# Scores of 64-feature heads: two heads at a time, one in each row half of TensorE's array, and attention rounds by pairs of heads

## The chip, the cores and the metric

The kernel runs on one core of one Trainium2 chip. The metric is the device time of one execution in microseconds (us). A core has TensorE (PE in the profile; PEld is its weight loads), VectorE (DVE), ScalarE (ACT), GpSimd (POOL) and SyncE (SP, whose queue issues the weight transfers).

## What is computed

The reference is two model blocks behind one another on x of 256 tokens by 1024 features, all in float32. Block one has two layers of: a gated norm, a mixer, a gated norm, a feed-forward part (width 2816). Block two has two layers of: half a feed-forward part, a mixer, attention on 256 memory tokens, half a feed-forward part. What matters here are the mixers whose heads have 64 features:

```python
# block one, both layers: 8 heads "slc" and 8 heads "win" share the queries; with 256 tokens
# both come to causal attention. 8 heads "moba" are causal attention too
s = einsum(q, k) * 64 ** -0.5        # 256 x 256 per head
p = masked_softmax(s, mask)
o = einsum(p, v)
# block two, layer 0: differential half (8 score maps, chunked mask) and stick half (8 heads)
p = p[:, :n_h] - lam * p[:, n_h:]
z = einsum(q, k) * 64 ** -0.5
later = cumsum(log_keep, reverse) - log_keep
w = where(strict, exp(log_sigmoid(z) + later), 0)
```

The other attention loops (block two, layer 1: 16 heads of 96 features; the memory attention: 4 heads of 128 features) are not by pairs in either kernel.

## The kernel before, in words

All five engines run one program each, written out by hand in program order; semaphores tie them. Every weight matrix is streamed in panels of 128 x 2048 elements through `ring` (3 slots). ScalarE copies a panel to the rounded part "hi" of `parts` (2 slots, L705), VectorE makes the rest "lo" by a subtraction (L2272, 128x2048), and TensorE multiplies hi by hi, hi by lo and lo by hi (L1489, L1495, L1497). A panel may be written to `parts` once TensorE has used the panel two before it. Panels of `w_ada` in between are not multiplied on TensorE: VectorE adds them up, four multiply-adds a panel (`ada_add`, L2281, `feat<-ring,scol,feat`), and TensorE sums the columns (`ada_cols`, L1507).

**The attention loops.** `head_steps` (L1674) gives TensorE three pieces per head: `scores` (two plain float32 products, of 128x128 and 128x256 outputs, L1686), `turn` (three 128x128 transposes of the probabilities, L1698) and `weighted` (probabilities by values, L1711). The loop of the first mixers (L1869) has 27 rounds. Round i does scores(i), turn(i-2), weighted(i-3) and then two steps of the weight products beside it (`more`, UNITS = 2; a step is 12 products of 512 columns or 24 of 256, and four steps use up a panel). Behind some rounds come extra pieces: the compressed branch (2, 5, 6), transposes of queries, keys and outputs (8, 14, 21), `ada_cols` (5, 9, 13, 17, 24, 26). The differential loop (L2029) has 11 such rounds with 2 or 3 steps. The stick loop (L2049) does in round i the score z(i) (L2053, L2055), the sums "later" of head i-1 (L2063 to L2065), the weighted values of head i-3 (L2078) and two steps.

**VectorE** in round i does first `masked(i)` (L2500: takes the scores out of PSUM, adds the mask, finds the row extreme `nmax`, which frees the bank), and then the rest of its round in program order: in even rounds the four multiply-adds of an ada panel and the lo of a weight panel, in some odd rounds head norms, rotations and branch sums. **ScalarE** in round i copies the transposed probabilities to `prob_t` (`turned_copy`), does `exps(i)`, and in odd rounds empties PSUM banks and makes a panel's hi.

**Banks and buffers.** Scores and transposes share two PSUM banks, `ATT = (0, 1)`; `open_bank` takes the one opened longest ago and waits until its last user has freed it. In the kernel before, scores take bank 0 and transposes bank 1 in every round. Masked scores lie in `shifted` (3 slots), transposed probabilities in `prob_t` (2 slots).

Heads n and n+1 of a pair have their queries and keys in the partitions 0 to 63 and 64 to 127 of the same tile:

```python
    q=nq_t[HD * g:HD * g + HD, j, :], k=k_t[HD * g:HD * g + HD, :]
    for i in range(HEADS + LAG + 1):
        if i < HEADS:
            scores(i)
```

## Time and profile before

| | us |
|---|---|
| median of 3 runs (lowest, highest) | 2058.11 (2057.46, 2058.28) |
| span of the profiled execution | 2056.4 |
| TensorE busy, matmuls | 2007.2 (98%) |
| TensorE busy, weight loads | 1779.3 (87%) |
| VectorE busy | 1463.2 (71%) |
| ScalarE busy | 1093.2 (53%) |
| mixer of block one, layer 0, attention loop | about 93 to 220 |
| the same, layer 1 | about 545 to 671 |
| differential loop, stick loop | about 1146 to 1190, 1198 to 1250 |

The profiled execution's own time is known by its span only, 2056.4 us; the runs' median is 1.7 us above it, about what lies around a span. In the rows below a line has the start in us from the span's start, the busy time of a merged group, the engine, the source line, the operation, output and inputs with their shapes, and the number of instructions. A plain float32 product shows as two matmuls, so one head's scores are four. In brackets stands the idle time of the engine ahead of the group and what ended it.

### The profile page before, as it was taken

What the parts mean: (1) busy time and instruction counts of PE and PEld (TensorE: products, weight loads), DVE (VectorE), ACT (ScalarE), POOL (GpSimd) and SP (SyncE); (2) the same over time, 40 slices, a digit from 0 to 9 for tenths busy, and PEclk for the clock granted to TensorE, in tenths of its full rate; (3) what the DMA queues carried; (4) which work ended last, traced back from release to release, by engine and by line L of the source; (5) the groups of instructions that cost most, each with busy time, mean ns of one, the idle gap of its engine ahead of it and who ended that gap; (6) DMA issues with size and microseconds to landing.
All of it is one profiled execution on the core that took longest, in us unless ns stands there. A gap on an engine that the chain in (4) does not pass through costs nothing. (4 is left out here: it accounts for less than half of the span.)

```text
span 2056.4 us, 32208 instructions
## 1 busy us (share of the span) xinstructions
PE 2007.2 (98%) x12956; PEld 1779.3 (87%) x12956; DVE 1463.2 (71%) x2322; ACT 1093.2 (53%) x1732; POOL 23.9 (1%) x46
## 2 busy tenths in 40 slices
PE   7999999999999999999999999999999999999999
PEld 4879988888889988898889779888898899899888
DVE  5888678867786686657766767677667757767774
ACT  3555545534655555545544665655445546855552
POOL 1001000000001000000000000000000000000000
PEclk9999999999999999999999999999999999999999
DMA  9555558867454466565556433455555554235554
GB/s 315 173 186 203 184 176 266 276 235 218 162 179 167 135 205 219 175 194 184 185 185 204 144 103 124 137 189 186 174 191 188 185 169 152 93 123 156 188 179 134
DMA packets 266212, 372.23 MB, mean 181 GB/s; under 512 B 8400, under 2 KB 160336, under 8 KB 266064
## 3 DMA queue, kind: packets, MB, share of 16 engines
q1 hardware_dynamic: 264736, 368.91, 55.1%
q8 instruction: 103, 1.69, 0.3%
q10 hardware_dynamic: 1328, 1.26, 0.2%
q14 instruction: 45, 0.37, 0.1%
HBM read 369.09 MB, written 1.05 MB: 180 GB/s over the span
## 5 line engine op out<-in xcount | busy, mean ns | idle before, releaser
L2272 DVE TENSOR_TENSOR parts<-ring,parts 128x2048 fp32r<-128x2048 f32 (+2 forms) x304 | 675.7, 2223 | 398.8 <-ACT parts L705 397.9
L705 ACT ACTIVATE parts<-ring 128x2048 fp32r<-128x2048 f32 (+2 forms) x304 | 565.5, 1860 | 577.6 <-PE psum L1497 317.1
L1497 PE MATMUL psum<-h,parts 128*128 128x512 f32 x1920 | 675.6, 397 | 0.0
L1495 PE MATMUL psum<-h,parts 128*128 128x256 f32 x1920 | 538.9, 281 | 0.3
L1497 PEld LDWEIGHTS psum<-h,parts 128*128 128x128 f32 x1920 | 360.5, 188 | 86.9
L1495 PEld LDWEIGHTS psum<-h,parts 128*128 128x128 f32 x1920 | 362.3, 189 | 2.5 <-DVE parts L2272 2.5
L1489 PE MATMUL psum<-h,parts 128*128 128x256 f32 (+1 forms) x2088 | 265.0, 285 | 4.5 <-DVE h L2281 2.0
L1489 PEld LDWEIGHTS psum<-h,parts 128*128 128x128 f32 (+1 forms) x2088 | 253.9, 190 | 7.3 <-issue 5.0
L1489 PE MATMUL psum<-parts,h 128*128 128x512 f32 (+1 forms) x864 | 204.4, 388 | 4.8 <-DVE parts L2272 3.4
L1489 PEld LDWEIGHTS psum<-hid_hl,parts 128*128 128x128 f32 x1584 | 189.5, 190 | 2.4 <-DVE parts L2272 2.4
L1489 PE MATMUL psum<-hid_hl,parts 128*128 128x256 f32 x1584 | 190.9, 283 | 0.8 <-DVE parts L2272 0.6
L1489 PEld LDWEIGHTS psum<-parts,h 128*128 128x128 f32 x864 | 155.1, 189 | 36.8 <-issue 4.6
L1497 PE MATMUL psum<-hid_hl,parts 128*128 128x512 f32 x528 | 186.8, 397 | 0.0
L1495 PE MATMUL psum<-hid_hl,parts 128*128 128x256 f32 x528 | 148.8, 282 | 0.1
L705 ACT ACTIVATE tok<-psum 128x512 f32<-128x512 f32 (+3 forms) x156 | 90.3, 579 | 70.9 <-PE psum L1497 61.8
L1497 PEld LDWEIGHTS psum<-hid_hl,parts 128*128 128x128 f32 x528 | 99.1, 188 | 24.3
L1495 PEld LDWEIGHTS psum<-hid_hl,parts 128*128 128x128 f32 x528 | 99.5, 188 | 0.6 <-DVE parts L2272 0.5
L705 ACT ACTIVATE scores_area<-scores_area,nmax 128x256 f32<-128x256 f32 (+1 forms) x160 | 72.2, 456 | 36.5 <-DVE nmax L2500 36.0
L2272 DVE TENSOR_TENSOR tok<-psum,tok 128x512 f32<-128x512 f32 x120 | 82.0, 683 | 1.9 <-ACT tok L705 1.7
L705 ACT ACTIVATE scores_area<-psum 128x384 f32<-128x384 f32 (+1 forms) x80 | 40.0, 499 | 77.3 <-PE psum L1698 76.9
L1686 PE MATMUL psum<-feat 64*128 64x128 f32 (+4 forms) x320 | 73.5, 351 | 1.5 <-DVE nmax L2500 0.9
L2500 DVE CUSTOM_DVE_ANT_0 scores_area<-psum,const,sums 128x128 f32<-128x128 f32 (+1 forms) x96 | 37.3, 426 | 52.5 <-PE psum L1686 48.3
(259 smaller groups left out, 2124.0 us busy)
## 6 DMA issues: line engine op xcount, KB each, us to landing
ring<-in_w_ada SPq DMA_DIRECT2D x48, 1024.0 KB, 5.3
ring<-in_w_ffn_in SPq DMA_DIRECT2D x88, 512.0 KB, 4.9
ring<-in_ffn_w_gate SPq DMA_DIRECT2D x88, 512.0 KB, 4.0
ring<-in_ffn_w_up SPq DMA_DIRECT2D x88, 512.0 KB, 5.0
ring<-in_w_in SPq DMA_DIRECT2D x36, 1024.0 KB, 5.1
ring<-in_ffn_w_down SPq DMA_DIRECT2D x32, 1024.0 KB, 5.1
ring<-in_w_ffn_out SPq DMA_DIRECT2D x16, 1024.0 KB, 5.1
ring<-in_ffn_w_down SPq DMA_DIRECT2D x16, 768.0 KB, 4.5
```

What stands on the lines that cost most here:

```text
L705: act.activation(out, in_, func, **kw).then_inc(*sig(name, *keys))
L1489: mm = pe.matmul(out, left, right, start=start and n == 0, stop=stop and n == 2, skip_group_check=True)
L1495: pe.matmul(bank[:, 0:S], wt_hl[1], act[:, 0, :], start=start, stop=False, skip_group_check=True)
L1497: return pe.matmul(bank.rearrange("p (a s) -> p a s", a=2), wt_hl[0], act, start=False, stop=stop, skip_group_check=True)
L1686: mm = pe.matmul(b[:, a:c], head["q"][:, P * t:P * t + P], head["k"][:, 0:c - a], start=True, stop=True)
L2272: dve.tensor_tensor(out, a, b, op).then_inc(*sig(name, *keys))
L2500: dve.tensor_tensor_reduce(to, of, add, times, 3.0e38, ALU.add, ALU.min, nmax[:, n % 3, t:t + 1]).then_inc(*sig("dve_nmax", *keys))
```

## The change

`scores` for heads of 64 features becomes `pair_scores`: it opens both `ATT` banks and issues the products of two heads alternately (first head 128 columns, second head 128, first 256, second 256). It runs in even rounds only. In a round the steps beside are divided: in even rounds both stand between the scores and `turn`, in odd rounds one ahead of `turn` and one behind `weighted`. `shifted` gets 4 slots in these loops and `nmax` 4 (the memory attention keeps 3 slots, by another division of the same area). ScalarE does `exps(i)` ahead of `turned_copy(i-2)`. The stick half issues z of two heads at a time. The loop of 96-feature heads keeps `scores`, with 4 slots and nothing else new.

```diff
-        shifted = scores_area[:, 0:3, :]
-        prob_t = scores_area[:, 3:5, :]
+        in_heads = scores_area.rearrange("p a n -> p (a n)")[:, 0:6 * 384].rearrange(
+            "p (a n) -> p a n", n=384)
+        shifted, prob_t = in_heads[:, 0:4, :], in_heads[:, 4:6, :]
...
+                    if i < HEADS:
+                        exps(heads[i], base + i,
+                             heads[i]["n"] + (8 if heads[i]["st"][0] == "win" else 0))
                     if LAG <= i < HEADS + LAG:
                         m = i - LAG
                         turned_copy(heads[m], base + m)
-                    if i < HEADS:
-                        exps(heads[i], base + i,
-                             heads[i]["n"] + (8 if heads[i]["st"][0] == "win" else 0))
...
+                def pair_scores(i):
+
+                    two = heads[i:i + 2]
+                    for key in (scores_need or {}).get(i, ()):
+                        pe.wait_ge(*at(key))
+                    banks = [open_bank(("scores", head["st"], head["i"]), ATT) for head in two]
+                    for t, (a, c) in enumerate(spans(two[0]["mask"])):
+                        for head, b in zip(two, banks):
+                            mm = pe.matmul(b[:, a:c], head["q"][:, P * t:P * t + P],
+                                           head["k"][:, 0:c - a], start=True, stop=True)
+                            if t:
+                                mm.then_inc(*sig("pe_scores",
+                                                 ("full", ("scores", head["st"], head["i"]))))
...
                 for i in range(HEADS + LAG + 1):
-                    if i < HEADS:
+                    if i < HEADS and i % 2 == 0:
                         scores(i)
+                    ahead = UNITS if i % 2 == 0 or i == 23 else 1
+                    advance(more, ahead)
                     if LAG <= i < HEADS + LAG:
                         turn(i - LAG)
-                    if i == 23:
-                        next(more, None)
                     if i > LAG:
                         weighted(i - LAG - 1)
-                    for n in range(UNITS - (i == 23)):
-                        next(more, None)
-                        if i == 2:
-                            compressed_scores(n)
+                    advance(more, UNITS - ahead)
...
                 for i in range(8 + LAG + 1):
-                    if i < 8:
+                    if i < 8 and i % 2 == 0:
                         scores(i)
+                    ahead = beside_diff(i) if i % 2 == 0 else 1
+                    advance(more, ahead)
...
-                    advance(more, beside_diff(i))
+                    advance(more, beside_diff(i) - ahead)
...
+                    if i < 8 and i % 2 == 0:
+                        banks = [open_bank(("z", i + j), stick if i else ATT) for j in range(2)]
+                        for k in range(2):
+                            for j in range(2):
...
-                if n >= 3:
-
-                    dve.wait_ge(*at(("full", ("turn", *att_log[n - 3]))))
+                if n >= slots(st):
+
+                    dve.wait_ge(*at(("full", ("turn", *att_log[n - slots(st)]))))
```

TensorE's program in the rounds 10 and 11 of layer 0, before. `h,parts` are steps, `psum<-feat` the scores, `psum<-const,scores_area` the transposes, `psum<-tok,scores_area` the weighted values; `dve_nmax` is the semaphore of `masked`:

```order
L1686 MATMUL psum<-feat 128x128 [waits dve_nmax]
L1686 MATMUL psum<-feat 128x256
L1698 MATMUL psum<-const,scores_area 128x128 [waits act_probs,act_copied]
L1698 MATMUL psum<-const,scores_area 128x128 [waits act_probs]
L1698 MATMUL psum<-const,scores_area 128x128
L1711 MATMUL psum<-tok,scores_area 128x64 [waits act_copied]
L1711 MATMUL psum<-tok,scores_area 128x64 x2
L1489 MATMUL psum<-h,parts 128x256 [waits dve_lo]
L1489 MATMUL psum<-h,parts 128x256 x23
L1686 MATMUL psum<-feat 128x128 [waits dve_nmax]
L1686 MATMUL psum<-feat 128x256
L1698 MATMUL psum<-const,scores_area 128x128 [waits act_probs,act_copied]
```

And the pair of rounds in the changed program:

```order
L1710 MATMUL psum<-feat 128x128 [waits act_copied]
L1710 MATMUL psum<-feat 128x128
L1710 MATMUL psum<-feat 128x256 x2
L1501 MATMUL psum<-h,parts 128x256 [waits dve_lo]
L1501 MATMUL psum<-h,parts 128x256 x23
L1724 MATMUL psum<-const,scores_area 128x128 [waits act_probs,dve_nmax]
L1724 MATMUL psum<-const,scores_area 128x128 [waits act_probs]
L1724 MATMUL psum<-const,scores_area 128x128
L1737 MATMUL psum<-tok,scores_area 128x64 [waits act_copied]
L1737 MATMUL psum<-tok,scores_area 128x64 x2
L1501 MATMUL psum<-h,parts 128x256 x12
L1724 MATMUL psum<-const,scores_area 128x128 [waits act_probs,dve_nmax]
```

The wait on `dve_nmax`, that is on `masked` having emptied the bank, has moved from the scores to the transposes: those of an even round need the pair's first head out of bank 0, those of an odd round its second head out of bank 1, and the scores now wait for ScalarE's copy (`act_copied`).

VectorE's program from `masked(8)` to `masked(9)` in the changed kernel. Its instructions stand in the same order as before in every round:

```order
L2530 ISA scores_area,nmax<-psum,const 128x256
L2530 ISA nmax 128x1
L2311 SCALAR_TENSOR_TENSOR feat<-ring,scol,feat 128x512 [waits dve_nmax,panel0]
L2311 SCALAR_TENSOR_TENSOR feat<-ring,scol,feat 128x512 [waits dve_ada] x3
L2302 TENSOR_TENSOR parts<-ring,parts 128x2048 [waits act_hi]
L2530 ISA scores_area,nmax<-psum,const 128x128 [waits pe_turned,pe_scores]
```

Nothing moved here: between the first and the second head of a pair VectorE still has the multiply-adds and the lo of a panel.

## Rows read from the trace of the kernel before

**Rows 1.** Profile page, part 1: busy time of each engine

```profile
PE 2007.2 (98%) x12956; PEld 1779.3 (87%) x12956; DVE 1463.2 (71%) x2322; ACT 1093.2 (53%) x1732; POOL 23.9 (1%) x46
```

**Rows 2.** Busy time by stretch: the mixer loops and the differential loop; columns named in the first line

```profile
core 0: us, PE busy (x) PEld busy (x) DVE busy (x) ACT busy (x) POOL busy (x), PEclk, DMA share, GB/s
93.00:220.00 127.00, 124.79 (x859) 107.27 (x858) 103.84 (x240) 69.23 (x169) 8.45 (x15) 1.00 0.56 193
545.00:671.00 126.00, 123.72 (x855) 106.83 (x854) 94.08 (x226) 69.76 (x170) 7.13 (x12) 1.00 0.49 168
1146.00:1190.00 44.00, 43.40 (x223) 33.58 (x221) 24.65 (x55) 27.82 (x64) 0.00 (x0) 1.00 0.43 144
```

**Rows 3.** Timeline, round 11 of layer 0: TensorE, and ScalarE's copy of the transposes

```profile
152.35 0.52 PEld L1686 LDWEIGHTS psum<-feat 64*128 64x128 f32 x4
152.35 0.92 PE L1686 MATMUL psum<-feat 64*128 64x128 f32 x4
153.20 0.55 PE L1698 MATMUL psum<-const,scores_area 128*128 128x128 f32 x3
153.59 0.78 PE L1711 MATMUL psum<-tok,scores_area 128*128 128x64 f32 x6
154.18 3.12 PE L1489 MATMUL psum<-h,parts 128*128 128x256 f32 x24
157.23 0.92 PE L1686 MATMUL psum<-feat 64*128 64x128 f32 x4
163.59 0.49 ACT L705 ACTIVATE scores_area<-psum 128x384 f32<-128x384 f32 x1 [2.62 <-PE psum L1698]
```

**Rows 4.** Timeline, TensorE: a head of 96 features in block two, layer 1

```profile
1762.16 0.82 PE L1686 MATMUL psum<-feat 96*128 96x128 f32 x4
1762.82 0.49 PE L1698 MATMUL psum<-const,scores_area 128*128 128x128 f32 x3
1763.15 0.78 PE L1711 MATMUL psum<-aux,scores_area 128*128 128x64 f32 x6
```

**Rows 5.** Timeline, VectorE, from `masked(12)` to `masked(13)` of layer 0

```profile
158.27 0.28 DVE L2500 CUSTOM_DVE_ANT_0 scores_area<-psum,const 128x128 f32<-128x128 f32 x1
158.82 0.08 DVE L2500 DVE_READ_ACCUMULATOR2_ANT nmax<- 128x1 f32 x1
159.01 3.12 DVE L2281 SCALAR_TENSOR_TENSOR feat<-ring,scol,feat 128x512 f32<-128x512 f32 x4
162.04 2.28 DVE L2272 TENSOR_TENSOR parts<-ring,parts 128x2048 fp32r<-128x2048 f32 x1
164.24 0.28 DVE L2500 CUSTOM_DVE_ANT_0 scores_area<-psum,const 128x128 f32<-128x128 f32 x1
```

**Rows 6.** Timeline, layer 0: VectorE's `masked(4)` and `masked(5)`, TensorE's scores(6)

```profile
113.94 0.29 DVE L2500 CUSTOM_DVE_ANT_0 scores_area<-psum,const 128x128 f32<-128x128 f32 x1 [1.98 <-PE psum L1686]
122.94 0.28 DVE L2500 CUSTOM_DVE_ANT_0 scores_area<-psum,const 128x128 f32<-128x128 f32 x1
123.49 0.08 DVE L2500 DVE_READ_ACCUMULATOR2_ANT nmax<- 128x1 f32 x1
123.63 0.92 PE L1686 MATMUL psum<-feat 64*128 64x128 f32 x4
```

**Rows 7.** Timeline, VectorE: an even round of layer 1 behind the last ada panel

```profile
641.88 2.28 DVE L2272 TENSOR_TENSOR parts<-ring,parts 128x2048 fp32r<-128x2048 f32 x1
646.00 0.35 DVE L2500 CUSTOM_DVE_ANT_0 scores_area<-psum,const,sums 128x128 f32<-128x128 f32 x1 [1.83 <-PE psum L1686]
```

**Rows 8.** Stick loop: z(6), z(5)'s bank, TensorE's wait, the stretch behind (rows 2's columns)

```profile
1229.13 0.70 PE L2053 MATMUL psum<-feat 64*128 64x256 f32 x2
1231.09 0.55 DVE L2272 TENSOR_TENSOR rot<-scores_area,psum 128x384 f32<-128x384 f32 x1
1232.38 0.93 PE L2063 MATMUL psum<-rot,const 128*128 128x256 f32 x2 [2.33 <-DVE rot L2272]
1232.30:1236.00 3.70, 3.62 (x14) 3.43 (x15) 3.54 (x8) 0.92 (x2) 0.00 (x0) 0.55 0.02 4
```

More of the change, by code:

```diff
@@ L299, in build @@
         rs = sb("rs", [P, 4, 8])
-        nmax = sb("nmax", [P, 3, TT])
+        nmax = sb("nmax", [P, 4, TT])
         sums = sb("sums", [P, 32, TT])
@@ L1693, in turn @@
                     b = open_bank(job, ATT)
-                    buf = shifted[:, (base + i) % 3, :]
+                    buf = shifted_of(head["st"], base + i)
                     for t, (a, c) in enumerate(spans(head["mask"])):
@@ L1710, in weighted @@
                         for n, o in enumerate(range(a, c, P)):
-                            mm = pe.matmul(head["o"][t], prob_t[:, (base + i) % 2, o:o + P],
+                            mm = pe.matmul(head["o"][t], prob_of(head["st"], base + i)[:, o:o + P],
                                            head["v"][n], start=n == 0, stop=o == c - P)
@@ L1714, in weighted @@
                         [("attended", head["st"])] if head["last"] else [])))
-                return scores, turn, weighted
+                return pair_scores if heads[0]["q"].shape[0] == HD else scores, turn, weighted
             pe.wait_ge(*at("loaded const"))
@@ L2049, in diff_mixer @@
                 for i in range(11):
-                    if i < 8:
-                        b = open_bank(("z", i), ATT if i < 2 else stick)
-                        r = slice(HD * (i % 2), HD * (i % 2) + HD)
-                        pe.matmul(b[:, 0:S], zk[r, i // 2, 0:P], zq[r, i // 2, :], start=True,
-                                  stop=True)
-                        pe.matmul(b[:, S:S + P], zk[r, i // 2, P:S], zq[r, i // 2, P:S],
-                                  start=True, stop=True).then_inc(
-                            *sig("pe_scores", ("full", ("z", i))))
+                    if i < 8 and i % 2 == 0:
+                        banks = [open_bank(("z", i + j), stick if i else ATT) for j in range(2)]
+                        for k in range(2):
+                            for j in range(2):
+                                r = slice(HD * j, HD * j + HD)
+                                mm = pe.matmul(banks[j][:, S * k:S * k + (P if k else S)],
+                                               zk[r, i // 2, P * k:P * k + P],
+                                               zq[r, i // 2, P * k:S], start=True, stop=True)
+                                if k:
+                                    mm.then_inc(*sig("pe_scores", ("full", ("z", i + j))))
                     if 1 <= i <= 8:
```

28 lines of the change are left out of this document (19 added, 9 removed).

## The prediction, as it was put on record

> **What bounds the kernel now.** I read the page's busy times first: TensorE's matmuls are busy for 98% of the span, VectorE 71%, ScalarE 53% [rows 1]. So a microsecond taken from TensorE counts as long as nothing else comes last. Then I read the busy times of three of the four loops that the change touches [rows 2]. In the loop of layer 0 TensorE is busy 124.8 of 127 us, but VectorE is busy 103.8, 82%, far over its mean; in layer 1 it is 94.1 of 126, in the differential loop 24.7 of 44. Last I read single rounds. A round of TensorE is 4.88 us (152.35 to 157.23): scores 0.85, transposes 0.39, weighted values 0.59, two steps 3.05 [rows 3]. VectorE is not in step with that. In an even round it has 0.63 of `masked`, then multiply-adds of 3.12 and a lo of 2.28, and only then `masked` of the next head: 158.90 to 164.24, 5.34 us in a row with no idle time [rows 5]. It holds because before, head 2m+1 has until the scores of head 2m+2.
>
> **What the change takes away: time in scores.** A head of 64 features takes 0.85 us from its first matmul to the transposes and 0.39 more to the weighted values, 1.24 in all [rows 3]; a head of 96 features with the same shapes takes 0.66 and 0.33, 0.99 [rows 4]. So entering and leaving the 64-row form costs 0.25 us, and about 0.09 more ahead of the first matmul in a merged row (my estimate from the same starts). One head in two no longer pays it, less 0.06 because a step and not a transpose follows: 0.28 us a pair. The four passes of a second head come on top, 0.66 if nothing overlaps. Its weight loads do not run beside each other: four loads are 0.52 busy, one load about 0.19, so they start 0.11 apart [rows 3]. If matmuls of different row halves may overlap, but start in order and each behind its load, the four passes of 128 columns still stand 0.11 apart; only of the four of 256 columns (0.22 each, from 0.66 less two of 0.11) two fall together. That gives 0.21. No row before shows two row halves in use at once, so the pair from its first matmul to its first step is bounded by 1.56 us (no overlap) and 1.0 us (one head and 0.15). I take **1.35**, the one that the rows of loads lead to. Where nothing waits, a pair saves 0.49 us, and 32 pairs (12 and 12, 4 differential, 4 stick) 15.7.
>
> By the Trainium skill (TensorE: Matmul & The Clock Gate, section The mechanism in Part 3) matmuls in different row groups start some 4 ns apart and run together; no row here shows it yet, and that is the end at 1.0.
>
> **What it adds: an earlier date for the second head.** The transposes of the odd round now go into bank 1, which holds the pair's second head until `masked(2m+1)`. From the pair's start T, TensorE asks for it at T + 1.35 + two steps 3.04 + transposes and values 0.93 + one step 1.52 = T + 6.84. Before, it asked at the second next scores, T + 9.75. VectorE sees the first head at T + 1.19 (last matmul of head one at T + 0.77, and 0.42 as between these two before) and has the second out at T + 1.19 + 0.63 + W + 0.64 + 0.05 = T + 2.5 + W, where W is its work in the even round. So **TensorE stalls as soon as W is over 4.3 us**, and W is 5.34 [rows 5]: a stall of 1.0 us, where 0.49 was won. Behind TensorE's wait on its queue stand the values, a step and the next pair, so VectorE gets its next first head late too; nothing makes the time good. ScalarE's copy of the transposes (0.49 [rows 3]) now stands behind `exps` of the late head; it is done 1.5 us after the turn starts, where the next pair asks after 2.4. That costs nothing, nor do the fourth slot and the new order on ScalarE; the DMAs are the same and on the same queue.
>
> Pair by pair, each W from VectorE's rows (delay against before, us):
> - Layer 0, pair 0-1: TensorE waits for `masked(1)` behind 5.1 us of work as before: 0. Pair 2-3: W 5.1, compressed scores beside: stall 1.1, delay 0.
> - Pair 4-5: W is 122.94 - 114.58 = 8.4 us, and scores(6) stood 0.06 behind `masked(5)` [rows 6]. Now the turn of round 5 stands there, and values, a step, `cmp turn` and `ada_cols`, 3.5 us, come behind it in place of ahead. Stall 4.2, delay 3.7.
> - Pairs 6-7, 8-9: the even rounds have 2.0 and 0.95 us of extra TensorE work, which cover W; delay falls to 2.4.
> - Pairs 10-11 to 22-23: W 5.3 to 5.8 in each, and 6.4 with `y_mix` in the last. Stalls of 0.9 to 1.4 (0.6 with the transposes of round 14), each less 0.49: +0.4, +0.6, +0.2, +1.0, +0.8, +1.0, +0.5. The loop ends 6.9 late.
> - Layer 1 is the same to round 17, 3.7 late there; behind the last ada panel W is 2.3 to 3.4 [rows 7], nothing stalls, and three pairs win 0.4 each: 2.4 late.
>
> Sum of the loops: +6.9 +2.4 = **+9.3 us**. In the same way it is +10.7 at 1.56 and +4.3 at 1.0.
>
> **Clock.** Behind a wait of 2.33 us the granted clock was 0.55 over the next 3.7 us, between its levels of 1.2 and 2.4 GHz [rows 8]. The two stalls of 4.2 us are longer. Such a stretch costs up to 1.7 us where TensorE is the bound; I take 1.5 each, **+3.0**.
>
> **Differential loop.** VectorE is busy 24.7 us in this loop's 10 rounds [rows 2], 2.5 a round with `masked` in it, so W stays under 4.3, and two or three steps cover it: nothing stalls, 4 x 0.49 = **-2.0** (-1.1 to -3.7).
>
> **Stick loop.** The first three pairs win about 1.4 us. The last z pair needs the bank of z(5), freed at about 1231.6 by 1231.09 and 0.55; z(6) alone was issued at 1229.13, ahead of the wait of 2.33 [rows 8]. It now stands behind it, 1.3 us of TensorE with a low clock: **0** (-1.5 to +1.5). The memory attention and the 96-feature loop change nothing.
>
> Sum: 9.3 + 3.0 - 2.0 + 0 = +10.3. The profiled span goes from 2056.4 to 2066.7, the median, 1.7 above it, from 2058.1 to **2068.4**. The case's own range: from 4.3 + 3.0 - 3.7 - 1.5 = +2.1 to 10.7 + 3.4 - 1.1 + 1.5 = +14.5, 2060 to 2073.
>
> **Rivals.**
> - *No overlap of the row halves*, so the change does only half of what it says: 1.56 a pair, +10.7 + 3.0 - 1.1 + 0.5 = +13, 2071. For it: no row shows an overlap. Against: nothing in the rows forbids it.
> - *Full overlap, as by the page named above*: 1.0 a pair. The loops give +4.3 (VectorE's chain remains), clock 3.0, differential -3.7, stick -1.5: +2.1, 2060, inside what cannot be told from no change.
> - *The other side: VectorE is in time.* The place is the turn of the odd round. If the second head is out before T + 6.8, because VectorE's work spreads into the idle time that it has ahead of `masked` elsewhere (1.83 us, for instance [rows 7]), every pair wins: -15.7 at 1.35, 2042; -9 with no overlap, 2049; with it in layer 1 and the late rounds alone, about -6, 2052. For it: VectorE is idle for 23 us of that loop [rows 2]. Against: its program order is fixed, and the idle time lies behind the second head, not ahead of it. It decides at W = 4.3 us.
>
> **Chances.** My case 0.40, no overlap 0.20, full overlap 0.14, VectorE in time 0.22, the rest (a new wait that I miss, slower still) 0.04. What a measurement can tell from no change is 0.2%, 4.1 us. Slower by more: 0.40 + 0.20 + 0.04, 0.64. Within: the full overlap, 0.14. Faster: 0.22. The range holds my case with its bounds and the milder half of the faster one: 2047 to 2073.
>
> **What would show it.** Right: in the loop of layer 0 TensorE's transposes wait for VectorE's `nmax` once in each pair, some 1 us each and about 4 us once in each layer, near round 5, with a half clock behind it; the loop ends some 7 us late; score pairs of about 1.3 us, the third and fourth loads ahead of the matmul; the differential loop 2 us shorter. Wrong: no wait of the transposes for VectorE; loops that end early; or pairs of 1.0 or 1.5 us, which tell the overlap. If VectorE's even rounds turn out shorter than 4.3 us, or the stalls are made good in the rounds 24 to 26, the forecast falls.

## The result, and the profile after the change

The changed kernel takes **2081.1 us** (median of four runs, 2077.7 to 2086.4), the kernel before on the same chip 2057.8 (2057.3 to 2058.3): a ratio of 1.0118 with a 95% interval from 1.0106 to 1.013. It is slower by 23.4 us, where 10.3 were forecast. The profiled execution took 2080.15 us, its span is 2078.3, 21.9 above the span before.

First the page's busy times, beside [rows 1], and the busy times of the three loops, beside [rows 2] (the same stretches on the clock of the span; the first line names the columns):

```profile
PE 1994.8 (96%) x12956; PEld 1778.5 (86%) x12956; DVE 1464.1 (70%) x2322; ACT 1094.7 (53%) x1732; POOL 23.7 (1%) x46
```

```profile
core 0: us, PE busy (x) PEld busy (x) DVE busy (x) ACT busy (x) POOL busy (x), PEclk, DMA share, GB/s
93.00:220.00 127.00, 112.44 (x788) 99.37 (x788) 95.41 (x226) 64.28 (x154) 8.36 (x15) 0.95 0.51 174
545.00:671.00 126.00, 113.38 (x765) 98.06 (x764) 90.87 (x226) 69.46 (x159) 7.04 (x12) 0.95 0.49 169
1146.00:1190.00 44.00, 40.52 (x207) 32.39 (x206) 35.77 (x70) 29.64 (x62) 0.00 (x0) 1.00 0.46 149
```

TensorE has 12.4 us less to do in all, although some of it ran at half clock, and takes 21.9 us longer over it. In the loop of layer 0 it is idle 14.6 us of 127, before 2.2, and its granted clock there is 0.95 on the mean, before 1.00.

A round of a pair, TensorE from pair 12-13 on; it answers to [rows 3]:

```profile
159.14 0.93 PE L1710 MATMUL psum<-feat 64*128 64x128 f32 x8
160.00 3.14 PE L1501 MATMUL psum<-h,parts 128*128 128x256 f32 x24
162.97 0.49 PE L1724 MATMUL psum<-const,scores_area 128*128 128x128 f32 x3
163.30 0.78 PE L1737 MATMUL psum<-tok,scores_area 128*128 128x64 f32 x6
```

Two heads now take 0.86 us from the first matmul to the step, as long as one took before. The eight matmuls of the group start in twos, 7 ns apart within a two, and the twos follow each other by 0.21, 0.11 and 0.21 us. The second head adds 0.01 us.

Now the turn of an odd round, which answers to [rows 5]: VectorE from `masked(14)` to `masked(15)` in layer 0, and TensorE's transposes behind it:

```profile
171.09 0.29 DVE L2530 CUSTOM_DVE_ANT_0 scores_area<-psum,const 128x128 f32<-128x128 f32 x1 [1.10 <-PE psum L1710]
171.95 0.49 DVE L2306 TENSOR_SCALAR feat<-ring,scol 128x512 f32<-128x512 f32 x1
172.47 2.98 DVE L2311 SCALAR_TENSOR_TENSOR feat<-ring,scol,feat 128x512 f32<-128x512 f32 x3
175.38 2.54 DVE L2302 TENSOR_TENSOR parts<-ring,parts 128x2048 fp32r<-128x2048 f32 x1
177.84 0.28 DVE L2530 CUSTOM_DVE_ANT_0 scores_area<-psum,const 128x128 f32<-128x128 f32 x1
178.53 0.55 PE L1724 MATMUL psum<-const,scores_area 128*128 128x128 f32 x3 [1.14 <-DVE nmax L2530]
```

And pair 4-5, against [rows 6]: the second head comes out 9 us behind the first.

```profile
112.39 0.29 DVE L2530 CUSTOM_DVE_ANT_0 scores_area<-psum,const 128x128 f32<-128x128 f32 x1 [2.11 <-PE psum L1710]
121.39 0.28 DVE L2530 CUSTOM_DVE_ANT_0 scores_area<-psum,const 128x128 f32<-128x128 f32 x1
122.09 0.79 PE L1724 MATMUL psum<-const,scores_area 128*128 128x128 f32 x3 [3.70 <-DVE nmax L2530]
```

The waits over the whole kernel (engine, line, what it waited for: us in total, times, the longest):

```profile
ACT scores_area L717 <- DVE nmax L2530: 89.1, 42, 5.1
PE psum L1724 <- DVE nmax L2530: 25.2, 18, 4.3
PE psum L1501 <- ACT aux L717: 7.2, 2, 3.6
```

The last of these is new in size: 7.2 us in two waits, one at the end of each block-one loop. The timeline there, layer 0; ScalarE has `exps` of head 23 late, then a table load, the gates' sigmoid and two copies, and TensorE's next step needs the bank that those copies free:

```profile
225.80 0.35 DVE L2530 CUSTOM_DVE_ANT_0 scores_area<-psum,const,sums 128x128 f32<-128x128 f32 x1 [0.17 <-DVE y_mix L2302]
226.60 0.40 ACT L717 ACTIVATE scores_area<-scores_area,nmax 128x128 f32<-128x128 f32 x1 [3.19 <-DVE nmax L2530]
227.98 1.28 ACT L717 ACT_TABLE_LOAD   x1
230.24 1.07 ACT L717 ACTIVATE aux<-psum 128x512 f32<-128x512 f32 x2
231.41 4.63 PE L1501 MATMUL psum<-y_mix,parts 128*128 128x256 f32 x24 [3.62 <-ACT aux L717]
```

Before, the same step waited 1.97 us in layer 0, and in layer 1 it hardly waited:

```profile
671.67 1.53 PE L1489 MATMUL psum<-y_mix,parts 128*128 128x256 f32 x11 [0.42 <-ACT aux L705]
```

Last, the clock. Three stretches of layer 0 in which TensorE was granted half its clock, 1.2 GHz in place of 2.4 (columns: TensorE busy, PEclk, DMA share, GB/s):

```profile
122.30:125.70 3.40, 3.40 (x14) 0.51 1.05 402
190.50:200.70 10.20, 10.20 (x50) 0.50 0.28 103
228.10:234.90 6.80, 3.50 (x16) 0.50 0.62 198
```

Before the change no stretch at half clock lay in the two loops of block one or right behind them; now there are seven, 40.8 us in all. The one at 122.3 stands behind the wait of 3.70 us. Ahead of the one of 10.2 us stands nothing but a row of short waits, 1.04, 1.21, 1.14 and 1.71 us, one in each pair.

Where the 21.9 us of the span are, measured between the first scores of each loop:

| | before | after | difference |
|---|---|---|---|
| start to the first scores of layer 0 | 93.6 | 91.9 | -1.7 |
| layer 0 to the first scores of layer 1 | 450.7 | 462.8 | +12.1 |
| layer 1 to the first differential scores | 602.1 | 613.9 | +11.8 |
| differential loop to the end | 910.1 | 909.7 | -0.3 |

The first line is no gain of the change: in the traces of this study it lies between 91.2 and 93.9 without regard to the kernel.

### The profile page after: what moved, and what is told of

It reads as the page before. It is cut to its first block, busy times and chain, and to the rows that moved or that the text cites. A ratio compares the mean times of both kernels' runs of the same rounds, so it can differ in the third digit from the quotient of the medians.

```text
span 2078.3 us, 32235 instructions
## 1 busy us (share of the span) xinstructions
PE 1994.8 (96%) x12956; PEld 1778.5 (86%) x12956; DVE 1464.1 (70%) x2322; ACT 1094.7 (53%) x1732; POOL 23.7 (1%) x46
## 4 chain that ended last, share of the span: by engine, by line
PE 74%; DVE 17%; ACT 5%; issue 3%; DMA 0%; DVEq 0%; ACTq 0%
PE psum L1501 29%; PE psum L1509 25%; PE psum L1507 13%; DVE parts L2302 6%; ACT parts L717 3%; DVE feat L2311 2%; PE psum L1737 2%; DVE scores_area L2530 1%; DVE tok L2302 1%; PE psum L1724 1%; PE psum L1710 1%; DVE rot L2302 1%; PE psum L1519 1%; DVE tok L2311 1%; DVE feat L2302 1%
## 5 line engine op out<-in xcount | busy, mean ns | idle before, releaser
L1501 PE MATMUL psum<-h,parts 128*128 128x256 f32 (+1 forms) x2088 | 273.1, 289 | 4.5 <-DVE h L2311 2.0
L1501 PEld LDWEIGHTS psum<-h,parts 128*128 128x128 f32 (+1 forms) x2088 | 259.2, 193 | 13.2 <-issue 8.3
L2530 DVE CUSTOM_DVE_ANT_0 scores_area<-psum,const,sums 128x128 f32<-128x128 f32 (+1 forms) x96 | 37.3, 426 | 52.5 <-PE psum L1710 33.1
L1724 PE MATMUL psum<-const,scores_area 128*128 128x128 f32 x248 | 41.8, 280 | 25.2 <-DVE nmax L2530 25.2
```

Source lines behind the costliest of these rows:

```text
L1501: mm = pe.matmul(out, left, right, start=start and n == 0, stop=stop and n == 2, skip_group_check=True)
L1724: mm = pe.transpose(b[:, o:o + P], buf[:, o:o + P], ident)
L2530: dve.tensor_tensor_reduce(to, of, add, times, 3.0e38, ALU.add, ALU.min, nmax[:, n % 4, t:t + 1]).then_inc(*sig("dve_nmax", *keys))
```

## The experiments

Theory one (the late second head): all of the loss comes from VectorE taking the second head only behind its multiply-adds and lo, with TensorE's turn waiting for it. Its rivals: the new frame costs by itself (steps ahead of the transposes, `exps` ahead of the copy on ScalarE, four slots); the half clock is the cause and not the waits; VectorE is simply full. Twelve kernels ran, in four groups, each group beside runs of the kernel before on the same chip; their medians were 2057.0, 2056.9, 2058.2 and 2057.8.

**Both heads at once on VectorE.** `both_masked` changes VectorE's order alone, in block one and in the differential loop:

```diff
-                    if i < HEADS:
-                        masked(heads[i]["st"], heads[i]["i"], con("causal"), HD ** -0.5)
+                    if i < HEADS and i % 2 == 0:
+                        for head in heads[i:i + 2]:
+                            masked(head["st"], head["i"], con("causal"), HD ** -0.5)
...
```

> The changed kernel, with VectorE taking both heads of a pair out of their banks back to back at the start of the even round (loops of block one and the differential loop), ahead of that round's multiply-adds and lo. Theory one, the late second head: TensorE's waits for VectorE at the turns (25.2 us of matmuls' idle time in the changed kernel) fall under 3 us, the 3.6 us waits behind ScalarE at the end of the two loops and the half clock in the loops go with them, and a pair then saves what one head's scores cost, some 0.8 us: 24 pairs in block one 19 us, with the differential loop 3, so 2036 us, between 2032 and 2042. Rival one, the frame (steps ahead of the transposes, exps ahead of the copy on ScalarE) costs by itself: waits of TensorE for ScalarE take the place of those for VectorE, 2055 to 2075. Rival two, VectorE becomes the bound, since 104 us of its work now stand in a loop of some 117: over 2045, with waits for its lo in even rounds.

Measured: 2045.7 us (2044.8 to 2046.4), ratio 0.9944 (0.9932 to 0.9957). One reordering on VectorE turns a loss of 23 us into a gain of 11. The waits of the turn for VectorE:

```profile
PE psum L1724 <- DVE nmax L2530: 0.3, 1, 0.3
```

A pair without waits, pair 10-11 of layer 0 (the next pair starts at 152.32, 8.79 us later; two rounds before took 9.74):

```profile
143.53 0.93 PE L1710 MATMUL psum<-feat 64*128 64x128 f32 x8
144.38 3.15 PE L1501 MATMUL psum<-h,parts 128*128 128x256 f32 x24
147.37 0.49 PE L1724 MATMUL psum<-const,scores_area 128*128 128x128 f32 x3
147.69 0.78 PE L1737 MATMUL psum<-tok,scores_area 128*128 128x64 f32 x6
```

So a pair takes 0.95 us off TensorE, 11.4 in a block-one loop. Theory one stands, and a frame that costs as much as the change lost falls. VectorE is not full either: the steps' waits for its lo are 6.4 us in the whole kernel, before 7.3. But the time is outside my range of 2032 to 2042: a layer gained 5.1 and 4.6 us, not 9.6, and the long waits behind ScalarE at the loops' ends, which I had expected to go, are still 2.38 us in layer 0 and 3.41 in layer 1. In layer 0, from 93 to 240 us, TensorE's idle time is 7.5 us, before 5.0, and behind two of its waits it ran at half clock. These are the two, a step of round 4 and the step at the loop's end:

```profile
112.13 1.19 PE L1501 MATMUL psum<-parts,h 128*128 128x512 f32 x2 [2.61 <-ACT sq L717]
212.09 1.19 PE L1501 MATMUL psum<-y_mix,parts 128*128 128x256 f32 x4 [2.38 <-ACT aux L717]
```

Added up: 11.4 us won, 2.5 lost in idle time, and half of the 8.5 us in which TensorE was busy at half clock, 4.2. That gives -4.7, measured -5.1. The same account, over the same stretch, for the changed kernel: 11.4 us won; 14.4 lost in idle time (19.4 in place of 5.0); and half of 17.1 us busy at half clock, 8.5. That gives +11.5, measured +12.1. The account says where the time is, not what each part would give back if it went alone: `warm_turn` below asks that for the clock.

**The order of the matmuls in a pair.** `serial_pair` is both_masked with both passes of head one ahead of those of head two:

```diff
-                    for t, (a, c) in enumerate(spans(two[0]["mask"])):
-                        for head, b in zip(two, banks):
+                    for head, b in zip(two, banks):
+                        for t, (a, c) in enumerate(spans(two[0]["mask"])):
```

> As both_masked, but the four matmuls of a pair go head by head (both passes of the first head, then both of the second) in place of turn by turn between the row halves. If the halves overlap only because neighbours in the queue use different halves (the trace of the changed kernel shows starts 7 ns apart inside each two), then here only the second and third matmul can run together: of two heads' passes, 0.11 + 0.22 + 0.11 + 0.22 us at two matmuls per head and twice that with float32's passes, some 0.2 to 0.4 us a pair comes back, 32 or 28 pairs, so 6 to 12 us more than both_masked. If the saving is all in entering and leaving the 64-row form once in two heads, the order makes no difference: within 2 us.

Measured: 2044.0 us (2043.1 to 2047.6), ratio 0.9941 (0.9928 to 0.9953): no difference from both_masked. The trace shows why, and it is not what the first of the two theories said. The matmuls of head two start 13 to 14 ns behind those of head one, in place of 7, and the group is as long, 0.86 us:

```profile
150.74 0.93 PE L1710 MATMUL psum<-feat 64*128 64x128 f32 x8
151.60 0.86 PE L1501 MATMUL psum<-h,parts 128*128 128x256 f32 x5
```

Head two does not wait for head one's second product, though it stands behind it in the program. In this kernel it is enough for the overlap that the two heads are neighbours on TensorE.

**A later turn.** `late_turn` is the changed kernel with both steps ahead of the transposes in odd rounds too:

```diff
-                    ahead = UNITS if i % 2 == 0 or i == 23 else 1
+                    ahead = UNITS
```

> The changed kernel, with both steps of an odd round ahead of its transposes (one step before). TensorE then asks for bank 1 some 1.5 us later. Theory one, the late second head: the repeated waits of 1.0 to 1.7 us at the turn go (VectorE's even work of 5.3 us now fits), the one of 4.3 us in each layer falls to about 2.7, and with them most of the half clock: 24 pairs win up to 0.8 us each, less 5 us for what stays, so 2045 us, between 2040 and 2055. The rival, that the waits are made by the whole period of VectorE's work and only move to another place: within 5 us of the changed kernel's 2081.

Measured: 2064.4 us (2061.4 to 2064.8), ratio 1.0032 (1.0019 to 1.0045). A miss, by 9 us beyond the range; the direction was right. The turn's waits fell as expected, but the pair's scores now wait in their place, and the wait at the loop's end stayed:

```profile
PE psum L1501 <- ACT aux L717: 7.2, 2, 3.6
PE psum L1724 <- DVE nmax L2530: 6.5, 10, 1.7
PE psum L1710 <- ACT feat L717: 2.4, 2, 1.2
PE psum L1710 <- DVE nmax L2530: 2.1, 2, 1.1
```

In layer 0, over the same stretch as above: 11.4 us won, 11.9 lost in idle time (16.9 against 5.0), and two half-clock stretches of 3.4 us, at most 3.4 us of loss; that gives up to +3.9, and the layer is 3.9 us longer than before. I had counted only the waits that I knew.

**The later loops alone.** `loops2_only` puts the first mixers' loop back as it was and gives its heads the old `scores`; differential and stick keep their pairs.

```diff
-                return pair_scores if heads[0]["q"].shape[0] == HD else scores, turn, weighted
+                return pair_scores if heads[0]["st"][0] == "diff" else scores, turn, weighted
...
-                    if i < HEADS and i % 2 == 0:
+                    if i < HEADS:
                         scores(i)
-                    ahead = UNITS if i % 2 == 0 or i == 23 else 1
-                    advance(more, ahead)
                     if LAG <= i < HEADS + LAG:
                         turn(i - LAG)
...
```

> Pairs in the differential and the stick loop alone; the first mixers' loops as before the change, head by head (with four slots, and exps ahead of the copy on ScalarE). By the traces the changed kernel's part from the differential loop on is as long as before within 0.4 us, so 2057.4, between 2055 and 2060, the same as before: all of the loss stands in the loops of block one. If ScalarE's new order or the slots cost by themselves in the first mixers, it shows here, at over 2060. If the half clock of the block-one loops has cost the later loops too, it is faster than before by 2 to 4 us.

Measured: 2059.9 us (2055.8 to 2061.6, eleven runs), ratio 1.001 (1.0001 to 1.0019). By its trace the layers take 450.7 and 601.7 us and the rest 911.0, against 450.6, 602.1 and 910.1. So the loss stands in the block-one loops, and neither the four slots nor ScalarE's order cost anything there. The pairs of the later loops win nothing either: the median is 2.9 us above the kernel before, at the edge of what the runs can tell, and from the first differential scores to the first z the loop takes 52.5 us, before 51.9.

**Block one alone.** `both_mix_only` is both_masked with differential and stick head by head; of the differential loop:

```diff
-                    if i < 8 and i % 2 == 0:
+                    if i < 8:
                         scores(i)
-                    ahead = beside_diff(i) if i % 2 == 0 else 1
-                    advance(more, ahead)
                     if LAG <= i < 8 + LAG:
                         turn(i - LAG)
                     if i > LAG:
                         weighted(i - LAG - 1)
-                    advance(more, beside_diff(i) - ahead)
+                    advance(more, beside_diff(i))
```

> both_masked in the loops of block one alone; the differential and the stick loop head by head, as before the change. By the traces of both_masked and of the kernel before, the part from the differential scores on is 909.0 and 910.1 us, so the pairs there are worth 1 us though they take 6 us of scores away: 2046.5, between 2044 and 2048.5, the same as both_masked. If the waits that both_masked shows there (2.24 and 1.57 us in the differential loop, 6 in the stick loop) cost more than the pairs win, it is faster than both_masked, 2042 to 2044.

Measured: 2045.1 us (2043.7 to 2047.0), ratio 0.9939 (0.9927 to 0.9952), the same as both_masked. The differential loop, from its first scores to the first z, is 51.9 us long in both and before the change. The trace of both_masked says where its four pairs lose what they win: the step behind the transposes waits, once for 2.24 and once for 1.57 us, 3.8 in all, as much as 4 x 0.95. ScalarE and TensorE around the first of them:

```profile
1148.11 0.49 PE L1724 MATMUL psum<-const,scores_area 128*128 128x128 f32 x3
1148.69 0.49 ACT L717 ACTIVATE scores_area<-psum 128x384 f32<-128x384 f32 x1 [2.92 <-PE psum L1724]
1149.48 1.25 ACT L717 ACTIVATE tok<-psum,rcol 128x512 f32<-128x512 f32 x2
1150.83 1.40 PE L1501 MATMUL psum<-parts,h 128*128 128x512 f32 x5 [2.24 <-ACT tok L717]
```

The steps had ended at 1148; their results could be copied out at once. But ScalarE has its copy of the transposes first in its program and sat idle for it for 2.92 us. Head by head, the transposes stood ahead of the steps, and the copies of results had scores, transposes and values as cover.

**One step ahead of the transposes.** `both_one_step` acts on that:

```diff
-                    ahead = UNITS if i % 2 == 0 or i == 23 else 1
+                    ahead = UNITS if i == 23 else 1
...
-                    ahead = beside_diff(i) if i % 2 == 0 else 1
+                    ahead = 1
```

> As both_masked, but TensorE takes one step, not two, between a pair's scores and the transposes of the even round (in block one and the differential loop), the other behind the weighted values. In the differential loop the two waits of 2.24 and 1.57 us that both_masked has at a step behind the transposes stand behind ScalarE's copies of the step results, which ScalarE's queue holds behind its copy of the transposes: with a step less ahead of the transposes this cover is back, and 3 to 4 us go there; a bank is asked for at 2.4 us from the pair's start, where masked(2m) has left it at about 1.9, so nothing is lost in block one. So 2042 us, between 2039 and 2045. If the waits are set by something else (the panels' arrival), 2045 to 2047; if the bank is late after all, TensorE waits for nmax in even rounds and it is over 2048.

Measured: 2046.2 us (2043.2 to 2048.5), ratio 0.9944 (0.9932 to 0.9957): the same as both_masked, and above the range. By the trace the gain in the differential loop is there, the part from its scores on is 906.5 us in place of 909.0. That nothing is lost in block one was wrong: layer 0 takes 447.2 us, and 443.7 to 445.6 in the traces that differ from both_masked in the later loops or the order of the matmuls alone; there are four waits of the transposes for nmax, 3.8 us in all, and the two products with the compressed weights in round 6 (L1927) wait 5.1 us, in both_masked 0.8. `both_diff_one` therefore takes one step in the differential loop alone, the second half of that diff:

> As both_masked, with one step in place of two between the pair's scores and the even transposes in the differential loop alone (block one keeps two). In both_one_step the part from the differential scores to the end was 906.5 us, in both_masked 909.0, while block one was slower with one step. If the two parts add, 2.5 us less than both_masked's 2045.7: 2043.2, between 2041 and 2045. If the gain in the differential loop was one profile's accident, 2045 to 2047.

Measured: **2042.7 us** (2042.4 to 2045.3), ratio 0.9931 (0.9919 to 0.9944). This is the lowest median of the study, 15 us below the kernel before, but its ratio's interval overlaps those of both_masked and `serial_pair`, so the runs alone do not tell the three apart. The traces do for the part that was changed: from the differential scores to the end it takes 906.3 to 906.5 us in the three kernels with one step there (this one, `both_one_step`, `both_diff_one_z`), 909.0 in both_masked and in `serial_pair`. The differential loop in its trace, TensorE busy for 42.0 of 44 us, where both_masked has 39.97 in the same loop:

```profile
1134.00:1178.00 44.00, 41.99 (x234) 33.47 (x234) 24.38 (x55) 29.24 (x65) 0.00 (x0) 1.00 0.44 144
```

`both_diff_one_z` puts the stick loop back to head by head in it:

```diff
-                    if i < 8 and i % 2 == 0:
-                        banks = [open_bank(("z", i + j), stick if i else ATT) for j in range(2)]
...
+                    if i < 8:
+                        b = open_bank(("z", i), ATT if i < 2 else stick)
...
```

> As both_diff_one, with the stick loop's scores head by head as before the change. In both_masked TensorE idles 6.0 us in the stick loop in four waits, three ahead of later (1.29, 0.51, 1.65) and one at the last pair of z (2.57); head by head, in both_mix_only, 3.5 us in three. A pair of z takes 0.9 us away, 3.6 in four pairs, and 2.5 of it come back as waits: the pairs of z win 1 us at most, so 2044, between 2042 and 2046, the same as both_diff_one. If the last z pair's wait and the half clock behind it weigh more, it is faster, 2041 to 2042.

Measured: 2045.0 us (2041.1 to 2045.6), ratio 0.9934 (0.9921 to 0.9948). The intervals lie on each other, and by the traces the part from the first z on is 856.3 us here and 856.5 with pairs; the pairs of z are worth nothing that can be measured.

**ScalarE's queue in round 3.** `both_cmp_late` moves the exps of the compressed scores behind ScalarE's steps of round 3 in both_masked, to free the copies that TensorE waits 2.61 us for:

```diff
-                    if i == 3:
-                        act.wait_ge(*at(("cmp shifted", l)))
-                        run(cmp_s, cmp_s, ACT.Exp, "act_step", ("cmp probs", l))
...
                     for _ in range(UNITS):
                         next(more, None)
+                    if i == 3:
+                        act.wait_ge(*at(("cmp shifted", l)))
+                        run(cmp_s, cmp_s, ACT.Exp, "act_step", ("cmp probs", l))
```

> As both_masked, but in round 3 of block one ScalarE takes the exps of the compressed scores behind its steps of that round, not ahead of them. In both_masked ScalarE stands from 107.1 to 109.7 us in the wait for VectorE's shifted compressed scores, with the copies of a finished step behind it, and TensorE's next step waits 2.61 us for those copies. If that queue order is the cause, TensorE gains up to 2.6 us in each layer, less what comes late behind it (VectorE's weights of the compressed branch, for the transposes of round 5): 2042, between 2040 and 2044.5. If VectorE is the bound in rounds 3 to 5 anyway, the same as both_masked within 1.5 us.

Measured: 2051.5 us (2046.8 to 2053.0), ratio 0.9966 (0.9954 to 0.9978). A miss, and 6 us worse. The wait of 2.61 us shrank to 0.65, but what comes behind, the product with the compressed weights in round 6, now waits:

```profile
PE psum L1927 <- ACT feat L717: 5.6, 2, 3.4
```

In both_masked these are 0.8 us. The transposes of the weights in round 5 do not wait. What is late is ScalarE's copy of them, since it stands behind the hi of a panel that has not landed:

```profile
125.30 1.91 ACT L717 ACTIVATE parts<-ring 128x2048 fp32r<-128x2048 f32 x1 [8.37 <-DMA ring<-in_w_in]
```

VectorE waited 1.36 us for the exps that had been moved, so its multiply-adds ended at 118.9 and not 117.8; the transfer of that panel is issued as they end, at 118.94 and 117.82, and landed at 125.3 and 123.1. A move in ScalarE's queue came back to it by way of VectorE and the ring.

**The clock by itself.** `warm_turn` is the changed kernel with fillers in the waits:

```diff
                     job = ("turn", head["st"], head["i"])
+                    if head["st"][0] in ("slc", "win", "moba") and i % 2 and i < 22:
+                        one = heads[i - 1]
+                        pe.wait_ge(*at(("copied", ("turn", one["st"], one["i"]))))
+                        warm(WARM_TURN, psum[:, tally.banks[("turn", one["st"], one["i"])], 0:256])
```

> The changed kernel, with 8 matmuls on idle data (0.12 us each, 0.9 in all) ahead of each turn of an odd round in block one, that is inside the waits for the second head; 22 turns in all. They fill about half of TensorE's idle time there. If the half clock behind those waits (41 us of it in and behind the loops of block one, 3.4 before the change) costs time by itself, the clock in these stretches rises and the kernel gains 5 to 15 us: 2066 to 2076. If VectorE's chain sets the pace of the pairs and a slow clock only eats into the wait, the clock rises and the time stays: 2078 to 2084. Where no wait is (the last pairs of layer 1) the fillers add 0.9 us each, 3 us in all at most.

Measured: 2080.2 us (2073.9 to 2082.0), ratio 1.0104 (1.0088 to 1.012), not to be told from the changed kernel. Half clock in and behind the two loops fell from 40.8 to 17.0 us, and the loop of layer 0 has none left:

```profile
91.00:219.00 128.00, 119.39 (x896) 103.99 (x896) 97.21 (x228) 67.51 (x163) 8.35 (x15) 1.00 0.53 181
```

Over the two pairs in which the changed kernel has its 10.2 us of half clock, from the scores of pair 16-17 (at 181.11 there, 182.03 here) to those of pair 20-21 (205.93, 204.08), this one takes 22.05 us against 24.82: about 2.8 us is what that stretch cost. Layer 0 is 1.9 us shorter and layer 1 0.1. So the half clock that the account above put at 8.5 us in layer 0 gives back far less when it goes: TensorE then waits longer for VectorE's chain, which sets the pace, as the waits left behind the fillers show (12.3 us still, for nmax). The fillers take time of their own where no wait covers them, so the clock's part may be somewhat larger than this.

**One pair at a time.** Last, two kernels that are the changed one but for a single pair of each layer, in which VectorE takes both heads together: pair 4-5 (`early_4`), with the longest wait, and pair 22-23 (`early_22`), at the loop's end.

```diff
-                    if i < HEADS:
-                        masked(heads[i]["st"], heads[i]["i"], con("causal"), HD ** -0.5)
+                    if i < HEADS and not (i % 2 and i - 1 in EARLY):
+                        for head in heads[i:i + 1 + (i in EARLY)]:
+                            masked(head["st"], head["i"], con("causal"), HD ** -0.5)
```

`EARLY` is `(4,)` in the one and `(22,)` in the other.

> The changed kernel, with VectorE taking both heads together in the pair 4-5 of each layer alone. It takes away the longest wait of each layer (3.70 and 4.28 us at the turn of round 5, on the first theory's largest term) and the half clock behind it; in their place both_masked shows 2.61 us at the step behind the pair. If the delay of a pair stays with all that follow, as the prediction took it, the loops end 1 to 2 us earlier each plus some 2 us of half clock in both: 2077, between 2073 and 2080. If later pairs only run to VectorE's own times, so that one wait less is given back as longer ones behind, no gain: 2080 to 2083.

Measured: 2074.5 us (2073.4 to 2081.0), ratio 1.0087 (1.0074 to 1.01).

> The changed kernel, with VectorE taking both heads together in the last pair, 22-23, of each layer alone. It tests the tail, which the prediction had at nothing: ScalarE's table load, sigmoids and copies stand behind the exps of head 23, and TensorE's next step waits 3.62 us for them in each layer, with 6.8 us of half clock behind. With head 23's exps earlier, the wait at the turn (1.23 us in layer 0, none in layer 1) goes and the 3.62 become 2.4 in each layer, as in both_masked: 3.7 us in all, 2077.5, between 2075 and 2080; with the half clock shorter too, 2072 to 2075. If the tail is set by something else, within 1.5 us of 2081.

Measured: 2076.5 us (2072.4 to 2078.5), ratio 1.0088 (1.0074 to 1.0102). The medians are 6.7 and 4.6 us below the changed kernel's, of the 35 us between it and both_masked, with ranges that just overlap its own (2077.7 to 2086.4).

The trace of `early_22` says that less than this is the pair's. With it the step at the loop's end of layer 0 waits 2.18 us in place of 3.62, and the wait of the turn ahead of it is gone (0.99 us for `y_mix` stands in its place). From the scores of pair 22-23 to the end of the steps on `y_mix` that makes 1.7 us in layer 0, and 0.2 in layer 1. Another 1.3 and 3.0 us of what its trace gains lie ahead of pair 22-23, where the program is the changed kernel's: between pair 8-9 and pair 22-23 this execution has 3.4 us of half clock in layer 0 and none in layer 1, where the changed kernel's has 10.2 and 6.8. In layer 1 the step at the end still waits 3.41 us, though `exps` of head 23 are done 1.55 us before ScalarE gets the transposes that its table load stands behind:

```profile
681.23 0.49 ACT L718 ACTIVATE scores_area<-psum 128x384 f32<-128x384 f32 x1 [1.55 <-PE psum L1725]
685.16 1.19 PE L1502 MATMUL psum<-y_mix,parts 128*128 128x256 f32 x4 [3.41 <-ACT aux L718]
```

So a late head 23 is not what makes this wait in layer 1. What is left is the new division of the rounds. Before the change both steps of round 23 and the transposes and values of round 24 stood between the transposes of round 23 and the step on `y_mix`, and covered ScalarE's chain; the wait was 0.42 us. Now the two steps stand ahead of the transposes of round 23, and those of round 24 behind the step on `y_mix`. It is the pattern of the differential loop again, but here it is read from the order alone; no kernel tried it.

The profile of `early_4` is of its slowest run, 2081.0 us, so its gain can't be read from it. But it shows where the wait can go. The 3.70 us at the turn of round 5 are gone, and in round 6 the product with the compressed weights waits instead, with 6.8 us of half clock around it. ScalarE's copy for it stands behind a panel again, for which ScalarE idles 7.08 us:

```profile
129.71 3.75 PE L1928 MATMUL psum<-feat 128*128 128x512 f32 x4 [3.43 <-ACT feat L718]
```

Pair 8-9 of layer 0 starts 46.5 us behind the loop's first scores, in the changed kernel 46.2. In layer 0 of that execution one wait less was given back by another, for a panel that VectorE's multiply-adds release no earlier than in the changed kernel (issued at 119.58 and 119.30). By what the four faster runs gained, no trace shows.

## Why the prediction was wrong

The direction, the mechanism and the place were right: TensorE's turn in odd rounds waits for VectorE's second head, in nine of the twelve pairs of layer 0 and seven of layer 1, mostly some 1 us and about 4 us near round 5. The sum was +10.3 and the span rose by 21.9. Layer 0 was forecast at 6.9 + 1.5 and measured at 12.1; layer 1, the largest miss, at 2.4 + 1.5 and measured at 11.8; the differential loop and what follows at -2.0 and measured at -0.3; the start of the kernel, by chance, gave back 1.7. Step by step:

- *"entering and leaving the 64-row form"; pair taken as 1.35 us.* Wrong: 0.86. What failed is the step "weight loads do not run beside each other": the first loads of the two halves start 7 ns apart. The full overlap that the Trainium skill states (TensorE: Matmul & The Clock Gate, section The mechanism in Part 3) is true here, with 7 ns where the page has 4. A pair saves 0.95 us, not 0.49. By the prediction's own sum for full overlap the forecast would have been +2.1, so this wrong term brought it nearer to the result, by luck.
- *"TensorE stalls as soon as W is over 4.3 us".* Right in form. With the pair at 0.86 both sides of the comparison come earlier: the turn of pair 10-11 is asked for at T + 6.4 (forecast 6.84), `masked(11)` is out at T + 7.4 (forecast 7.8), a stall of 1.04 us (forecast 1.0). Those of the later pairs of layer 0 were 1.1 to 1.7 (none in pair 18-19) against 0.9 to 1.4. A pair that waits for VectorE keeps nothing of what its scores save.
- *"Stall 4.2, delay 3.7" at pair 4-5.* The waits were 3.70 and 4.28 us. At pair 6-7 layer 0 stood 5.3 us behind, forecast 3.7 and 1.5 for the clock, so 5.2; layer 1 stood 6.9 behind.
- *Clock, "The two stalls of 4.2 us are longer ... I take 1.5 each".* Wrong in number. There were seven, and the longest, 10.2 us, came behind short waits that repeat. It cost about 2.8 us by `warm_turn`; half clock behind short stalls was in no term of the sum. From pair 10-11 up to there the pairs lost 0.3 to 0.5 us each, forecast 0.2 to 0.6; in the two pairs with this stretch they lost 2.6 and 1.9, forecast 1.0 and 0.8.
- *The loops' end, costed at nothing ("the loop ends 6.9 late").* Wrong, and the largest single omission. At the last pair layer 0 was 10.0 us late and layer 1 7.0; at the end of the steps on `y_mix` they were 13.2 and 11.8. So 3.2 and 4.8 us came behind the last pair's scores, where I had looked at VectorE and TensorE and not at ScalarE's queue: table load, sigmoid and copies stand there behind the copy of the transposes, TensorE's step waits 3.62 us for them (before 1.97 and 0.42), and a half clock of 6.8 us follows in each layer. Late `exps` of head 23 are a part of it in layer 0, where `early_22` gains 1.7 us, and 0.2 in layer 1. The rest fits the steps moved ahead of the transposes, which no run put back.
- *"Layer 1 ... three pairs win 0.4 each: 2.4 late."* It was 7.0 late at the last pair: the longer stall, and a half clock of 6.8 us across the pairs 16-17 and 18-19. The first of them lost 2.4 us, the second 0.7 instead of winning 0.4. The same program in `early_22` has no half clock there and was 4.0 late, so about 3 us of this term differ from one execution to the next.
- *Differential loop, -2.0 ("nothing stalls").* From its first scores to the first z the loop came out 0.7 us longer. VectorE stalled it once, for 0.43 us; ScalarE did by 3.8 us, because the steps had been moved ahead of the transposes while ScalarE's copies of their results stayed behind the copy of the transposes. The term counted VectorE's work alone.
- *Stick loop, 0.* Right within its range: the part from the first z to the end is 1.0 us shorter, and the last pair of z waits, 2.58 us, with a half clock of 3.4 us behind it.

The rival "VectorE is in time" is what `both_masked` makes true by another order. It would then have been forecast at -15.7; the measured gain was 11.

## What to carry to other kernels

When two jobs are fused on one engine, both results need a taker at the same time: look at the program order of the engine that empties the second buffer, and move that work with it. The same edit was 23 us slower without this and 11 us faster with it. Where a step is moved, follow it through every queue, that of the engine that copies its result and that of the transfers too, and through the end of the loop. And a bound engine with 1 us of waiting in each round can lose more than the waits: in layer 0 its clock followed them down for 10.2 us, which cost about 2.8.

## What the hardware showed that I had not expected

- Float32 matmuls on the two row halves of the array run fully beside each other, weight loads included: eight matmuls in 0.86 us where four took 0.85. Their order in the program made no difference to the time: head by head they start 13 to 14 ns apart, in turn 7 ns.
- Waits of 1.0 to 1.7 us, one in each 10 us or so of otherwise busy time, were followed by 10.2 us at 1.2 GHz in layer 0, as the single wait of 3.70 us was by 3.4. With fillers in the waits, that stretch was at full clock. It is not the same in each execution: `early_22`, with the same program up to there, has 3.4 us in place of the 10.2.
- The changed kernel's runs spread over 8.8 us where the kernel before spreads over 1.0 in the same group. The spread goes with the clock: the mean granted clock of its four runs, from the fastest (2077.7 us) to the slowest (2086.4), is 0.990, 0.988, 0.987 and 0.985. Which of the two makes the other was not tried.
